# Sliding-window attention computed among the even mixer's input products

## What is computed

```
q, k, v, g, lr, sq, sk, sv = split(h @ w_in)          # 256,256,512,512,16,512,128,128 columns
o_a = gated linear attention(q, k, v, decay from lr @ w_a2 + b_a), normed, times silu(g)
o_b = sliding-window attention(sq, sk, sv): 8 query heads, 2 key heads of 64;
      a chunk of 64 tokens sees its own and the 2 chunks before (192 keys),
      softmax(logits / 8 + relative bias, with one sink logit per head) @ values
out = concat(o_a, o_b) @ w_out
```

## Time and profile before

| | |
|---|---|
| three timed runs | 4105.18, 4107.73, 4112.48 (median 4107.73) |
| profiled execution | 4104.21, its span 4102.3 |
| TensorE busy | 3551.3 of 4102.3 (87%), mean granted clock 0.932 |
| VectorE, ScalarE, GpSimd busy | 1543.5, 1123.8, 611.9 |
| input products and gate, SyncE's first issue to that of `gla_prep` | 130.45 to 410.96 |
| mixer A | 410.96 to about 590 |
| `swa`, SyncE's first issue to ScalarE's first of `split` | 590.74 to 760.02 |

### The profile page before, as it was taken

One profiled execution on the slowest core, in us unless ns is written; L12 is line 12 of the kernel. 1 busy time (PEld: TensorE's weight loads), 2 busy tenths in 40 slices (PEclk: granted clock), 3 DMA queues, 4 the chain that ended last, 5 costly groups with the idle time before them and its releaser, 6 DMA issues. The chain is left out here.

```text
span 4102.3 us, 62461 instructions
## 1 busy us (share of the span) xinstructions
PE 3551.3 (87%) x26609; PEld 3333.2 (81%) x26609; DVE 1543.5 (38%) x2368; ACT 1123.8 (27%) x2085; POOL 611.9 (15%) x877
## 2 busy tenths in 40 slices
PE   9887546798799999999889987476897799999998
PEld 8886433597699999999569877464896799999998
DVE  6211425433333223223524649545424333233233
ACT  6100233321232112112534542243312222121123
POOL 2000210010021001012121238430100111010011
PEclk9998778999899999999789999788899899999999
DMA  6321111122111111111554665874222211111111
GB/s 226 101 78 54 59 43 25 35 63 88 53 43 46 47 47 47 47 47 37 169 187 153 227 202 148 199 169 110 52 70 66 63 47 47 47 47 47 47 43 62
DMA packets 486248, 347.33 MB, mean 85 GB/s; under 512 B 117358, under 2 KB 459342, under 8 KB 482734
## 3 DMA queue, kind: packets, MB, share of 16 engines
q1 hardware_dynamic: 455658, 314.48, 27.0%
q0 software_dynamic: 10368, 19.51, 1.5%
q10 hardware_dynamic: 19956, 9.49, 0.9%
HBM read 244.65 MB, written 98.85 MB: 84 GB/s over the span
## 5 line engine op out<-in xcount | busy, mean ns | idle before, releaser
L79 PE MATMUL ps<-ff_h,ff_wh 128*128 128x352 f32 x4224 | 1009.3, 322 | 0.0
L79 PEld LDWEIGHTS ps<-ff_h,ff_wh 128*128 128x128 f32 x4224 | 730.3, 188 | 1.3
L79 PE MATMUL ps<-y_parts,ff_wh 128*128 128x352 f32 x2880 | 695.3, 323 | 16.3 <-DVE ff_wl L1504 16.3
L79 PE MATMUL ps<-ff_h,ff_wl 128*128 128x352 f32 x2112 | 676.5, 320 | 0.0
L79 PEld LDWEIGHTS ps<-y_parts,ff_wh 128*128 128x128 f32 x2880 | 504.8, 189 | 16.6 <-DVE ff_wl L1504 16.6
L79 PE MATMUL ps<-y_parts,ff_wl 128*128 128x352 f32 x1440 | 466.2, 324 | 0.0
L79 PEld LDWEIGHTS ps<-ff_h,ff_wl 128*128 128x128 f32 x2112 | 396.0, 187 | 0.0
L79 PE MATMUL ps<-rw_parts,rw_wh 128*128 128x352 f32 (+1 forms) x1152 | 290.0, 334 | 23.5 <-PEq L2937 13.0
L1888 POOL TENSOR_TENSOR ff_silu<-ff_silu,rs 128x352 f32<-128x352 f32 x132 | 126.9, 963 | 1229.4 <-ACT ff_silu L1827 1229.4
L1648 DVE TENSOR_TENSOR x<-ps,x 128x352 f32<-128x352 f32 x240 | 126.0, 525 | 485.1 <-PE ps L79 482.3
L79 PEld LDWEIGHTS ps<-y_parts,ff_wl 128*128 128x128 f32 x1440 | 272.1, 189 | 0.0
(11 more groups left out here) (388 smaller groups left out, 5667.3 us busy)
## 6 DMA issues: line engine op xcount, KB each, us to landing
ff_w<-in_ffn_w SPq DMA_DIRECT2D x120, 512.0 KB, 3.8
mixed_t<-oq_st SPq DMA_DIRECT2D x48, 176.0 KB, 1.9
rw_ra_d<-tb_rk SPq DMA_DIRECT2D x8, 1056.0 KB, 8.0
rw_kbt_d<-tb_gk SPq DMA_DIRECT2D x8, 1056.0 KB, 4.0
rw_gg_d<-tb_gk SPq DMA_DIRECT2D x8, 1056.0 KB, 6.8
fr_w<-in_xa_wk SPq DMA_DIRECT2D x8, 1024.0 KB, 5.4
fr_w<-in_xa_wv SPq DMA_DIRECT2D x8, 1024.0 KB, 5.3
oq_w<-in_xa_wq SPq DMA_DIRECT2D x16, 512.0 KB, 4.1
```

The lines of the kernel that those rows point to most:

```text
L79: mm = nc.tensor.matmul(out, l, part, start=start and n == 0, stop=stop and n == 2)
```

## The change

`product`, `turn_out`, `swa_keys`, `swa_bias`, `swa` and `gate_product` are gone. A new function `even_products` does all their work in one block, in this order of units: keys, values (units 0 and 1), four units of queries (2 to 5), the 16 gate columns (6), and then the 12 units of mixer A (7 to 18). Keys, values and queries stay in SBUF (`ext`, `q`). From unit 7 on, TensorE works by half groups (12 matmuls of 352 columns, one block and four steps of K); after every fourth one, it takes a bunch of small products: the transposes of the last chunk's probabilities (`turns`), the scores of the next chunk and its values' transposes (`scores`), and the last chunk's product with the values (`meets`). The scores take the two key heads apart, 64 rows and 64 columns each, without the zero blocks. The three banks 0 to 2 take the sums (a ring of 3, so a bank must be emptied before the next unit's same block), banks 3 to 7 the attention. ScalarE issues the weight loads. Mixer A follows, and `split` of `y` becomes two blocks of four rows, since o_a and o_b are now two tensors.

The core of the diff (of `even_products` its TensorE part and the main loops of VectorE and ScalarE):

```diff
+def even_products(nc, ps, a, o, h, rs, ab, gate, y, ident):
+    w = a["ab_w_in"][0]
+    wk = w.rearrange("(k p) n -> p k n", p=P)
+    table_d = nc.dram_tensor("bias_table", (SWA_HEADS, CHUNK * (KEYS + CHUNK)), F32, kind="Internal").ap()
+    GLA0, NG, N = 7, 12, SWA_CHUNKS
+    wide_ = KEYS + CHUNK
+    def load_sq(dst, u):
+        return [(dst[:, :, 0:HD], wk[:, :, ROW_SQ + u * HD:ROW_SQ + (u + 1) * HD]),
+                (dst[:, :, HD:P], wk[:, :, ROW_SQ + (u + 4) * HD:ROW_SQ + (u + 5) * HD])]
+    units = [(lambda dst, r=r: [(dst, wk[:, :, r:r + P])], KT) for r in (ROW_SK, ROW_SK + P)]
+    units += [(lambda dst, u=u: load_sq(dst, u), KT) for u in range(4)]
+    units.append((lambda dst: [(dst[:, :, 0:GLA_LR], wk[:, :, ROW_LR:ROW_LR + GLA_LR])], KT))
+    units += [(lambda dst, u=u: [(dst, wk[:, :, u * P:(u + 1) * P])], KT) for u in range(NG)]
...
+        groups = Groups(nc, ctx, "ab", ps, units, BLK, BLOCKS)
+        weights = groups.weights
...
+        halves = (slice(0, HD), slice(HD, P))
+        at = lambda c: EXT_CACHE if c == N - 1 else c * CHUNK
+        scores_at = lambda i: (i - 1) // 4 if i % 4 == 1 and (i - 1) // 4 <= N else None
+        HALVES = 6 * NG
...
+            def gate_tile(n):
+                u, blk = n // BLOCKS, n % BLOCKS
+                pe.wait_ge(gate_in, 32)
+                groups.wait_emptied(pe, 6, blk)
+                if n >= BLOCKS:
+                    pe.wait_ge(gate_out, n - BLOCKS + 1)
+                elif n == 0:
+                    pe.wait_ge(new_copied, 4)
+                nc.tensor.matmul(ps[:, 5 + n % BLOCKS, 0:BLK], b[:, u * P:(u + 1) * P], low[:, columns(blk)], start=True,
+                                 stop=True).then_inc(gates, 1)
+            def scores(c):
+                if c == 0:
+                    pe.wait_ge(cached, 1)
+                    pe.wait_ge(row_set, 1)
+                    pe.wait_ge(cleared, 3)
+                    for blk in range(BLOCKS):
+                        groups.wait_emptied(pe, 5, blk)
+                else:
+                    pe.wait_ge(biased, c)
+                    pe.wait_ge(v_copied, c)
+                for p in range(4):
+                    for r in halves:
+                        nc.tensor.matmul(ps[r, 3 + p // 2, p % 2 * KEYS:(p % 2 + 1) * KEYS],
+                                              q[r, p, c * CHUNK:(c + 1) * CHUNK],
+                                              ext[r, 0, at(c):at(c) + KEYS], start=True, stop=True)
+                nc.tensor.transpose(ps[:, 3, 2 * KEYS:2 * KEYS + P], ext[:, 1, at(c):at(c) + P], ident[:])
+                nc.tensor.transpose(ps[0:CHUNK, 4, 2 * KEYS:2 * KEYS + P], ext[:, 1, at(c) + P:at(c) + KEYS], ident[:])\
+                    .then_inc(scored, 1)
+            def turns(c):
+                pe.wait_ge(probs, c + 1)
+                if c:
+                    pe.wait_ge(p_copied, c)
+                else:
+                    pe.wait_ge(gate_out, 2 * BLOCKS)
+                for p in range(4):
+                    nc.tensor.transpose(ps[:, 5, p * P:(p + 1) * P], sc[:, c % 2, p, 0:P], ident[:])
+                for p in range(4):
+                    mm = nc.tensor.transpose(ps[0:CHUNK, 6, p * P:(p + 1) * P], sc[:, c % 2, p, P:KEYS], ident[:])
+                mm.then_inc(p_turned, 1)
+            def meets(c):
+                pe.wait_ge(p_copied, c + 1)
+                pe.wait_ge(v_copied, c + 1)
+                if c:
+                    pe.wait_ge(o_out, c)
+                both = pt[:].rearrange("r (p k q) -> r k p q", p=4, k=2)
+                both2 = pt2[0:CHUNK, :].rearrange("r (p k q) -> r k p q", p=4, k=2)
+                for k, r in enumerate(halves):
+                    nc.tensor.matmul(ps[r, 7, 2 * P:4 * P], vt[:, c % 2, r], both[:, k], start=True, stop=False)
+                for k, r in enumerate(halves):
+                    mm = nc.tensor.matmul(ps[r, 7, 2 * P:4 * P], vt2[0:CHUNK, c % 2, r], both2[:, k], start=False, stop=True)
+                mm.then_inc(o_done, 1)
+            for j in range(GLA0):
+                for blk in range(BLOCKS):
+                    groups.sum(pe, j, blk, h)
+                if j == 0:
+                    prelude()
+                if j == 2:
+                    turn_new()
+            for i in range(HALVES):
+                j, blk, part = GLA0 + i // 6, i // 2 % BLOCKS, i % 2
+                groups.sum(pe, j, blk, h, part * KT // 2, (part + 1) * KT // 2)
+                c = scores_at(i)
+                if c:
+                    turns(c - 1)
+                if c is not None and c < N:
+                    scores(c)
+                if c:
+                    meets(c - 1)
+                if i in (2, 3):
+                    for n in range(BLOCKS):
+                        gate_tile(BLOCKS * (i - 2) + n)
...
+            def bend(dst, j, blk, rows_=slice(0, P)):
+                groups.wait_summed(dve, j, blk)
+                return groups.frees(nc.vector.tensor_tensor(dst, groups.bank(j, blk)[rows_, :], rs[rows_, columns(blk)], ALU.mult),
+                                    j, blk)
+            def prelude():
...
+            for j in range(GLA0):
+                if j:
+                    weights.low(dve, j + 1)
+                for blk in range(BLOCKS):
+                    if j < 2:
+                        keys(j, blk)
+                    elif j < 6:
+                        bend(q[:, j - 2, columns(blk)], j, blk)
+                    else:
+                        bend(low[:, columns(blk)], j, blk, slice(0, GLA_LR))
+                if j == 0:
+                    prelude()
+                if j == 2:
+                    copy_new()
+                if j == 4:
+                    vary()
+            for i in range(HALVES):
+                j, blk = GLA0 + i // 6, i // 2 % BLOCKS
+                if i % 6 == 0:
+                    weights.low(dve, j + 1)
+                if i % 2:
+                    if j > GLA0:
+                        dve.wait_ge(stored[blk], 16 * (j - GLA0))
+                    bend(stage[:, blk], j, blk)
+                c = scores_at(i)
+                if c is not None and c < N:
+                    before(c)
+                c = scores_at(i - 2)
+                if c:
+                    leave(c - 1)
+                if c is not None and c < N:
+                    after(c)
...
+            nc.scalar.preload_act_table_set(LN_EXP)
+            weights.load(act, 0)
+            weights.load(act, 1)
+            weights.high(act, 0)
+            weights.high(act, 1)
+            def gate_tile(n):
+                u, blk = n // BLOCKS, n % BLOCKS
+                act.wait_ge(gates, n + 1)
+                if n == 0:
+                    act.wait_ge(gate_in, 32)
+                nc.scalar.activation(y[:, 2 + u, columns(blk)], ps[:, 5 + n % BLOCKS, 0:BLK], ACT.Identity, bias=bcol[:, u:u + 1])\
+                    .then_inc(gate_out, 1)
+            def exps(c):
+                s = c % 2
+                act.wait_ge(negated, 2 * c + 2)
+                for p in range(4):
+                    nc.scalar.activation(sc[:, s, p], sc[:, s, p], ACT.Exp, bias=ng[:, s, p:p + 1], accum_out=lsum[:, s, p:p + 1])
+                nc.scalar.activation(es[:, s], es[:, s], ACT.Exp).then_inc(exped, 1)
+            def turned(c):
+                act.wait_ge(p_turned, c + 1)
+                nc.scalar.activation(pt[:], ps[:, 5, :], ACT.Copy)
+                nc.scalar.activation(pt2[0:CHUNK, :], ps[0:CHUNK, 6, :], ACT.Copy).then_inc(p_copied, 1)
+            for j in range(GLA0):
+                if j:
+                    weights.high(act, j + 1)
+                weights.load(act, j + 2)
+            for i in range(HALVES):
+                j = GLA0 + i // 6
+                if i % 6 == 0:
+                    weights.high(act, j + 1)
+                    weights.load(act, j + 2)
+                c = scores_at(i)
+                if c:
+                    turned(c - 1)
+                if c is not None and c < N:
+                    exps(c)
+                if i in (2, 3):
+                    for n in range(BLOCKS):
+                        gate_tile(BLOCKS * (i - 2) + n)
```

```diff
 def even_layer(nc, ps, a, o, x, rs, ident, ones, ab, gate, mixed, cols):
-    w = a["ab_w_in"][0]
-    wk = w.rearrange("(k p) n -> p k n", p=P)
-    with nc.cleanup_on_exit(), nc.sbuf_tensor("h0", [P, 2, KT, TOK], F32R) as h2:
-        h = (h2[:, 0], h2[:, 1])
-        with nc.cleanup_on_exit():
-            front(nc, ps, a, o, x, h, rs, ident, ones)
-        product(nc, ps, "qkvg", 12, KT, plain(w), h, ("store", rows(ab)), rs)
-        def load_sq(u, dst):
-            return [(dst[:, :, 0:HD], wk[:, :, ds(u * HD + ROW_SQ, HD)]),
-                    (dst[:, :, HD:P], wk[:, :, ds(u * HD + (ROW_SQ + 4 * HD), HD)])]
-        product(nc, ps, "sq", 4, KT, load_sq, h, ("store", rows(ab, R_SQ)), rs, per_load=2)
-        product(nc, ps, "skv", 2, KT, plain(w, ROW_SK), h, ("store", rows(ab, R_SK)), rs)
```

(17 more changed lines are left out.)

580 lines of the change are left out of this document (163 added, 417 removed).

## The result

The changed kernel takes **3964.36 us** (median of four runs, 3961.41 to 3967.64) against 4109.1 for the kernel before (four runs, 4105.18 to 4112.48): ratio 0.9648, 95% interval 0.9632 to 0.9665. The profiled executions went from 4104.21 to 3961.41, so 142.8 us where the prediction's sum had 131.6, and 3964 where it had 3976, inside its range.

The account below looks back on a forecast made before the run. TensorE, busy 87% of the span, was taken as the bound. Terms -169.3 + 1.8 + 35.9 = -131.6 us took the profiled 4104.2 us to 3972.6, or 3976 for the median of timed runs; range 3958 to 4011.

Parts of the forecast that it names:

- What bounds the kernel: Whole kernel: TensorE, busy 87% of the span, no other engine above 38%; time goes only where TensorE gains.
- The attention stage goes, -169.3: Separate attention stage after mixer A: its removal saves 169.3 us; DRAM trips for bias and cache rows cost nothing under units 0 to 5.
- Split of y, +1.8: Split of y before the output product: two blocks instead of one add 1.8 us to 10.55 us.
- The stretch, +35.9: Input products, now with attention among them: 316.4 us instead of 280.5, 35.9 us more.
- Start 7.5: Start of the stretch: 6.2 us from first load to first matmul plus a 1.28 us table load ahead of the loads.
- Nineteen units of 11.65 and the cold beginning 2.3: Sums of the stretch: 19 units at 11.65 us, 221.3 us, plus 2.3 us for the first, partly at lower clock.
- Bunches 74.6: Attention work among the sums: first bunch 1.9 us, sixteen whole at 4.3 us, last 3.9 us, together 74.6 us.
- VectorE's chain costs nothing: Softmax chain between bunches: probabilities ready at about 10.5 us, 12.0 with a unit's split, of a 12.1 us period; no cost.
- Rival 1: Scores and values' products in the bunches: the array halves do not overlap, TensorE pays 35 us, 4011; chance 16%.
- Rival 2: Bunches: VectorE's queue delivers probabilities 0.5 to 2 us late, +3 to +34 us, about 3990; chance 13%.
- Rival 3: Stretch of products: cheaper through complete overlap and free switches, or a shorter tail, 3962; chance 5%.
- Rival 4: Stretch from unit 7 on: waits in the bunches drop TensorE to its lower clock, 4187; chance 1.5%.

Follow-up runs that it names:

- no_bunches: Changed kernel without any bunch: no scores, softmax or products with the values, o_b filled with zeros, so attention is not computed; 3889.31 us, ratio 0.9470.
- full_passes: Changed kernel with scores as whole-array passes, one per head pair instead of two quarter passes, queries unpadded so logits differ from the reference; 3953.05 us, ratio 0.9625.
- every_two: Changed kernel with a bunch after every second half group instead of every fourth, the softmax's second part following at once; 3976.29 us, ratio 0.9686.
- every_three: Changed kernel with a bunch after every third half group instead of every fourth, the softmax's second part following at once; 3965.93 us, ratio 0.9660.
- attention_last: Changed kernel with all 19 units of sums first, then the 18 bunches one after the other in the same block; 4069.99 us, ratio 0.9915.
- half_after_half: Changed kernel with a bunch's scores ordered as all four passes of key half 0, then all four of half 1, instead of in turn; 3974.64 us, ratio 0.9667.
- merged_only: Kernel before with only its three product calls and gate product merged into one block of 19 units, attention still its own stage; 4055.51 us, ratio 0.9875.

## Why the prediction was right, by its own steps

- **What bounds the kernel.** Right: where sums and bunches alternate, TensorE is busy 189.21 of 190 us at clock 1.00.
- **The attention stage goes, -169.3.** Right, and its DRAM trips cost nothing under the first units: TensorE has no wait there.
- **Split of y, +1.8.** It was +1.5: 631.24 - 618.50 = 12.74 against 11.22.
- **The stretch, +35.9.** It was +27.9 (308.4 against 280.5), and here lie 8 of the 11 us by which the gain was underestimated. By terms:
  - *Start 7.5*: 6.8, from 131.24 to 138.00. The step "a table load that now stands ahead of the loads in ScalarE's queue" failed: the loads are issued 0.03 us after the table load begins.
  - *Nineteen units of 11.65 and the cold beginning 2.3*: a block of a unit takes 3.84 us (144.80 to 148.64), 11.5 a unit, so 0.13 less each, 2.5 us in all; the first unit, 14.5 us to its last eviction for 14.1 before, takes back 0.4.
  - *Bias lookup and new rows 1.5*: 1.1. *Gate tiles 4.7*: twice 2.04 less the last pass's latency, 3.9. *Tail 4.5*: 4.2.
  - *Bunches 74.6*: 1.9 + 16 x 3.95 + 3.4 = 68.5; no_bunches gives 70.7 with every effect around them. This is the term that was mis-sized most, by 3.9 us, and two errors in it partly cancel. The overlap was taken at 0.58 and 0.6 of serial, and it is complete: half of serial. The changes of form were taken at 0.4 us a bunch, and they cost about 0.7. Passes alone are 0.87 us for eight transposes, 1.30 for the scores, 0.22 for the values' transposes and, as an estimate from 0.163 us per 192 columns, 4 x 0.22 = 0.87 for the values' products, 3.26 where the prediction had 3.9; the bunch of 3.95 leaves 0.7 for five changes, 0.14 each, as full_passes has it (0.15). The forecast's 1.5 for the scores, measured 1.45, is so right by luck: 1.30 and a change of form. The last bunch waits 1.2 us for ScalarE and not 1.6.
- **VectorE's chain costs nothing.** Right, and narrowly so in the chunks with a split, by 0.2 us. From a bunch's start the probabilities are ready after 10.3 us, with a split after 11.5, for 10.5 and 12.0 forecast (the 8.9 on the way there is 2.8 + 5.9 = 8.7). every_two and every_three show the chain to be 8.80 us when nothing stands in it, so that the 10.5 and 12.0 us were made by the kernel's own order, which puts `after` behind the third half group, and were slack that could be had.
- **Rival 1, no overlap (4011).** Excluded: pairs of passes start at once, and less overlap costs time, 2.15 us against 1.45. Its price was well sized. Without any overlap the scores would need 8 more steps of 0.16 us, 1.3 us, and the values' products 1.14, so a bunch of 6.4 us where the bound had 6.3. The rival's doubt, that passes of 192 columns share less than ones of 64, did not come true: a pair costs one pass.
- **Rival 2, VectorE's queue.** Did not happen; it begins below a period of 8.8.
- **Rival 3, a cheaper stretch (3962, 5%).** This is where the time fell, 2 us from its value and 12 from the forecast's. The bound named there gives 3976 - 10 = 3966, the other 4 us of its value are worked out from nothing, and the tail was only 0.3 us shorter. Its condition came half true: the overlap is complete, but the changes of form are not free. That the time comes out so near is in part luck, since the start, the units, the gate tiles and 3 us of unchanged stages have a share as large.
- **Rival 4, the clock.** Did not happen among the sums; in attention_last it does, at TensorE's 4.7 us idle in 10.25.
- The remaining 3 us (2.8 behind the output product's load, 1.0 in mixer A, less 0.8 in a later start of the stretch) are of the size by which unchanged stages differ between executions. Nothing here says they belong to the change.

## What to carry to other kernels

A chain of small dependent operations costs TensorE only its own passes when sums fill the period, provided that the period is longer than the chain: here 8.8 us at the least, 10.3 to 11.5 in the order of the changed kernel. Place inside a bunch what needs no result between two steps that hand over through another engine, order passes so that neighbours have the same form in different corners or sides of the array, and count the changes of form, 0.15 us each here: a padded whole pass may be cheaper than two quarters beside each other. After such a move the next gain lies in the remaining gaps between blocks: 13.3 us in two layers from loads and a split that start a block earlier were more than the 5 us that the form of the scores was worth.

## What the runs showed of the hardware that was not expected

- A pass of 64 rows, 64 columns and 192 moving columns takes as long as a whole one, 0.16 us (half_after_half, 316.12 to 316.28; 1.30/8 in full_passes). Two in opposite corners start at once and cost one (311.85, two passes).
- Overlap does not need strict turns: with all passes of one corner first, the other corner's began beside the last four of them (two starts at 316.44).
- Going into the form of 64 rows and 64 columns and out of it costs 0.15 us each way (0.30 a bunch in full_passes). Between transposes that write 128 partitions and ones that write 64, no such cost shows (311.32 - 310.88 = 0.44 for four, 0.11 each).
- Opposite corners write one PSUM bank at the speed of two banks: 1.45 us either way.
- Two products of 256 columns on different column sides and with equal rows take 0.58 us together, as long as one alone. If the row count changes between them, they do not overlap, on different sides either (319.31 to 319.88).
- A load issued by ScalarE's queue starts 0.03 us after an ACT_TABLE_LOAD of 1.28 us, beside it, and lands no later: its split begins 4.4 us after the issue (131.24 to 135.63), 4.3 in merged_only (132.87 to 137.19), which has no table load there.
- After 4.7 us of idle time the eight transposes of a bunch ran at half speed (1.90 us for 0.97, granted clock 0.50), and by its values' transposes the bunch was at its usual pace (1.00). With about 1 us of idle time in every 8.8, in every_two, the granted clock stayed 1.00.
